# Token projections by strips of 256 x 512, attention probabilities normalised at the output, and two moved waits in a two-layer hybrid backbone kernel

## The reference

```python
p = h @ w_in[li]                                   # one projection for all mixers
def diff_softmax(q, k, v, lam):
    s = einsum('bhqcd,bhkcd->bhcqk', q, k) * (A_DQK ** -0.5)
    p = softmax(s, axis=-1)
    a = p[:, :, 0] - lam * p[:, :, 1]
    return einsum('bhqk,bhkv->bhqv', a, v)
y = rmsnorm(o, subln_w) * (1.0 - lambda_init)      # after attention
mod = silu(c) @ w_ada[li] + b_ada[li]              # shifts, scales and gates
```

## Time and profile before

| what | value |
|---|---|
| median of 3 runs | 2313.76 us (2312.54 to 2314.17) |
| profiled execution, own time | 2313.24 us |
| its span in the profile | 2311.2 us |
| PE, busy share of the span | 94% |
| DVE, ACT, POOL | 51%, 37%, 29% |
| token projections, matmuls of 256 columns | 1344 |

### The profile page before, as it was taken

One profiled execution on the slowest core, in us unless ns is written; L12 is line 12 of the kernel. 1 busy time (PEld: TensorE's weight loads), 2 busy tenths in 40 slices (PEclk: granted clock), 3 DMA queues, 4 the chain that ended last, 5 costly groups with the idle time before them and its releaser, 6 DMA issues.

```text
span 2311.2 us, 36487 instructions
## 1 busy us (share of the span) xinstructions
PE 2171.6 (94%) x13284; PEld 1822.6 (79%) x13284; DVE 1167.6 (51%) x1937; ACT 861.9 (37%) x1655; POOL 671.4 (29%) x607
## 2 busy tenths in 40 slices
PE   6998999999998999999899999899999889998999
PEld 3565788898664888887788888678889767998999
DVE  4745444435567332335543443454555565557665
ACT  2334333232552332333332231354333444444443
POOL 2432222246122111114320123433335433114120
PEclk8999999999999999999999999999999989999999
DMA  7412333322652123233223333220002423554554
GB/s 234 144 46 100 103 99 110 110 93 83 205 183 80 36 92 100 94 96 92 81 92 100 95 97 100 78 73 19 20 19 66 133 69 100 174 178 143 182 182 146
DMA packets 233362, 245.36 MB, mean 106 GB/s; under 512 B 11475, under 2 KB 230036, under 8 KB 232212
## 3 DMA queue, kind: packets, MB, share of 16 engines
q1 hardware_dynamic: 229648, 232.19, 31.9%
q10 hardware_dynamic: 3588, 11.49, 1.4%
HBM read 237.36 MB, written 6.29 MB: 105 GB/s over the span
## 4 chain that ended last, share of the span: by engine, by line
PE 71%; DVE 11%; issue 8%; ACT 4%; POOL 4%; DMA 1%; DVEq 0%; SPq 0%; ACTq 0%; POOLq 0%
PE psum L562 50%; PE psum L557 20%; DVE big L2028 5%; DVE big L2037 2%; PE psum L681 2%; POOL whl L1274 1%; ACT tmp L1478 1%; ACT big L1478 1%; POOL big L2721 1%; DMA raw<-in_w_ada_dram 1%; DVE big L2032 1%; ACT whl L1265 1%; POOL big L2615 1%; ACT big L1481 1%; DVE small L2429 1%
## 5 line engine op out<-in xcount | busy, mean ns | idle before, releaser
L562 PE MATMUL psum<-hhl,whl 128*128 128x512 f32 (+1 forms) x4416 | 828.7, 347 | 27.6 <-DVE hhl L2149 18.4
L562 PEld LDWEIGHTS psum<-hhl,whl 128*128 128x128 f32 x4416 | 702.7, 192 | 154.2 <-issue 43.7
L1265 ACT CAST whl<-raw 128x512 fp32r<-128x512 f32 x656 | 374.3, 618 | 884.7 <-PE psum L562 879.8
L1274 DVE TENSOR_TENSOR whl<-raw,whl 128x512 fp32r<-128x512 f32 x480 | 330.6, 730 | 487.2 <-ACT whl L1265 486.6
L557 PE MATMUL psum<-big 128*128 128x128 f32 (+5 forms) x2944 | 484.4, 328 | 31.9 <-DVEq L1246 13.1
L562 PE MATMUL psum<-bigr,whl 128*128 128x512 f32 (+1 forms) x2688 | 470.0, 336 | 4.7 <-DVEq L2534 2.5
L557 PEld LDWEIGHTS psum<-big 128*128 128x128 f32 (+2 forms) x2944 | 383.1, 195 | 109.4 <-issue 49.7
L562 PEld LDWEIGHTS psum<-bigr,whl 128*128 128x128 f32 x2688 | 414.3, 190 | 57.9 <-issue 4.7
L1274 POOL TENSOR_TENSOR whl<-raw,whl 128x512 fp32r<-128x512 f32 x176 | 230.1, 1329 | 400.5 <-ACT whl L1265 381.7
L1481 ACT COPY big<-psum 128x512 f32<-128x512 f32 (+1 forms) x330 | 184.7, 560 | 292.5 <-PE psum L557 199.8
L2028 DVE TENSOR_TENSOR big<-big,psum 128x512 f32<-128x512 f32 (+1 forms) x166 | 99.2, 598 | 148.0 <-PE psum L557 143.9
(11 more groups left out here) (148 smaller groups left out, 1455.4 us busy)
## 6 DMA issues: line engine op xcount, KB each, us to landing
raw<-in_w_mlp_dram SPq DMA_DIRECT2D x128, 512.0 KB, 3.6
raw<-in_w_ada_dram SPq DMA_DIRECT2D x96, 512.0 KB, 4.6
raw<-in_w_in_dram SPq DMA_DIRECT2D x88, 512.0 KB, 3.6
raw<-in_w_gate_dram SPq DMA_DIRECT2D x64, 512.0 KB, 3.5
raw<-in_w_branch_dram SPq DMA_DIRECT2D x32, 512.0 KB, 3.5
raw<-in_w_o_dram SPq DMA_DIRECT2D x16, 512.0 KB, 3.5
hy_spectra<-big SPq DMA_DIRECT2D x2, 2560.0 KB, 8.5
big<-hy_spectra ACTq DMA_DIRECT2D x2, 1280.0 KB, 5.7
```

What stands on the lines that cost most here:

```text
L562: m = nc.tensor.matmul(o_, a(p_), b(q_), start=first and i == 0, stop=last and i == 2, skip_group_check=shared)
L1265: nc.scalar.copy(whl[:, r, 0, ks], raw_of(n)[:, ks]).then_inc(S["hi_ready"], 1)
L1274: ins = eng.tensor_tensor(whl[:, r, 1, ks], raw_of(n)[:, ks], whl[:, r, 0, ks].bitcast(F32), ALU.subtract)
```

## The change

It has four parts. **First**, a strip of a token projection now has 256 rows and all 512 columns; it is loaded, cast and split in the same two halves of 512 columns. Each matmul moves 512 columns, a projection still takes four strips, and each unit holds one token tile. All units of a projection are opened at its first strip and end in its last one, tile by tile. ACT copies the first three tiles (or all but the last) before the cast that follows the last strip, and the last tile behind it; the woven pieces' two copies both come with the fourth piece. `half_way` runs after the second strip. **Second**, `combine` makes the sum of the first exponential times its factor over that of the second, so that the first exponential stays undivided. The division by its sum is made in `o_copy`, in four ACTIVATE instructions with a scale by head in place of one copy, after a new DVE reciprocal of four sums (`inverse_ready`). **Third**, layer 1's rows go to a part of `rstd`, with a semaphore of their own, and are turned to columns in group 2 of the modulation; DVE copies those columns after `filter_cut(0, 1)`. **Fourth**, in layer 1 POOL waits for `eo_ready` of the second convolution before it makes the low parts for `merge`.

The diff, cut to its core (callers that only lose an argument, DVE's side of `columns`, and the removed bodies of `token_strips` and `woven_piece` are left out):

```diff
...
 modrow = rows[:].rearrange("p a c -> p (a c)")
+rows_of = [rows, None]
...
 rstd = sb("rstd", [P, T])
+rows_of[1] = rstd[:, 0:2 * P].rearrange("p (a c) -> p a c", a=2)
...
-ROWS_DONE = [7 * 16, 12 * 16]
+ROWS_DONE = [7 * 16, 5 * 16]
...
-PAIRS = [(0, 1), (1,)]
+def by_rows(w, off):
+    return [w[STRIP * j:STRIP * (j + 1), off:off + BR_W].rearrange("(k p) n -> p k n", p=P) for j in range(4)]
+def token_tiles(li, key):
+    return range(2, NT) if li and key in ("dz", "aq") else range(NT)
+def add_tokens(key, li, off):
+    n = len(token_tiles(li, key))
+    add(key, li, by_rows(w_in[li], off), [1, 1, 1, n], n)
...
-    np_ = len(PAIRS[li])
...
-        add(key, li, by_columns(w_in[li], off, 512), [1, np_] * 2, 2 * np_)
-    add("ak", li, by_columns(w_in[li], OFF_AK, 512), [1, 2] * 2, 4)
-    add("av", li, by_columns(w_in[li], OFF_AV, 512), [1, 2] * 2, 4)
+        add_tokens(key, li, off)
+    add_tokens("ak", li, OFF_AK)
+    add_tokens("av", li, OFF_AV)
...
+    token_banks = []
+    def token_strip(key, li, j):
+        tl = token_tiles(li, key)
+        assert first_strip[key, li] + j == n_strip[0]
+        w = strip().rearrange("p q (k a) n -> p q k (a n)", k=2)
+        if j == 0:
+            token_banks.clear()
+        for i, m_ in enumerate(tl):
+            if j == 0:
+                token_banks.append(unit())
+            for k in range(2):
+                m = mm3(token_banks[i], lambda p_: hhl[:, p_, 2 * j + k, m_ * P:(m_ + 1) * P],
+                        lambda q_: w[:, q_, k, :], j + k == 0, j == 3 and k == 1)
+            if j == 3 or m_ == NT - 1:
+                m.then_inc(unit_done, 1)
+    def token_strips(key, li):
+        assert first_unit[key, li] == n_unit[0]
+        for j in range(4):
+            token_strip(key, li, j)
...
+        token_strip(key, li, n)
...
+    def columns(li):
+        pe.wait_ge(rows_loaded[li], ROWS_DONE[li])
+        b = fill(("cols", li))
+        nc.tensor.transpose(b[:, 0:100], rows_of[li][0:100, 0, :], ident[0:100, 0:100])
+        n = 52 if li == 0 else 36
+        nc.tensor.transpose(b[:, 128:128 + n], rows_of[li][0:n, 1, :], ident[0:n, 0:n]).then_inc(filled, 1)
...
-        for li in range(DEPTH):
-            pe.wait_ge(rows_loaded, ROWS_DONE[li])
-            if li == 0:
-                pe.wait_ge(consts_loaded, 16)
-            b = fill(("cols", li))
-            nc.tensor.transpose(b[:, 0:100], rows[0:100, 0, :], ident[0:100, 0:100])
-            n = 52 if li == 0 else 36
-            nc.tensor.transpose(b[:, 128:128 + n], rows[0:n, 1, :], ident[0:n, 0:n]).then_inc(filled, 1)
+        pe.wait_ge(consts_loaded, 16)
+        columns(0)
...
                 filter_taps(0, 1)
+                columns(1)
...
-    per = {"dz": len(PAIRS[li]), "aq": len(PAIRS[li])}.get(key, 2)
-    return first_mark[key, li] + (1 + per) * (i // per) + 2 + i % per
+    if key in ("dz", "aq", "ak", "av"):
+        return first_mark[key, li] + 4 + i
+    return first_mark[key, li] + 3 * (i // 2) + 2 + i % 2
...
+def exp_sum(m_, h, cc):
+    c0 = SUMC + (8 + h % 2 if cc else 4 * (m_ % 2) + h)
+    return small[:, c0:c0 + 1]
+def exp_inverse(m_, h, n=1):
+    c0 = SUMC + 12 + 4 * (m_ % 2) + h
+    return small[:, c0:c0 + n]
...
+        to = rows_of[li]
+        for dst, src in ((to[0:48, 0, :], b_ada[li]), (to[48:56, 0, :], norm1[li]),
+                         (to[56:64, 0, :], norm2[li]),
+                         (to[64:100, 0, :], hy_conv[li].rearrange("a c -> (a c)")),
+                         (to[0:36, 1, :], dn_conv[li].rearrange("a c -> (a c)"))):
+            sp.dma_start(dst, src.rearrange("(r c) -> r c", c=P)).then_inc(rows_loaded[li], 16)
...
+            sp.dma_start(rows[36:44, 1, :], c_ctx.rearrange("(r c) -> r c", c=P)).then_inc(rows_loaded[li], 16)
+            sp.dma_start(rows[44:52, 1, :], c.rearrange("a (r c) -> (a r) c", c=P)).then_inc(rows_loaded[li], 16)
...
                 sp.wait_ge(S["lo_ready"], split_no[last] + 1)
-        sp.dma_start(raw_of(n), strips[n]).then_inc(strip_loaded[at % RAW], 16)
+        dst = raw_of(n)
+        if strips[n].shape[1] == 2:
+            dst = dst.rearrange("p (k a) n -> p k (a n)", k=2)
+        sp.dma_start(dst, strips[n]).then_inc(strip_loaded[at % RAW], 16)
...
-                if n % 2:
-                    b = unit_bank_of(act, key, li, n // 2)
-                    dst = dz_tok[:, 2:4] if key == "dz" else y[:, ATT, 0:2]
-                    step(copy(dst[:, :, n // 2 * STRIP:(n // 2 + 1) * STRIP],
-                              b.rearrange("p (m n) -> p m n", m=2)),
-                         act_step if key == "dz" else S["token_copied"])
-                    give_unit(act, key, li, n // 2)
+                for u, m_ in enumerate(tiles(li)) if n == 3 else ():
+                    b = unit_bank_of(act, key, li, u)
+                    if key == "dz":
+                        step(copy(dz_tok[:, m_, :], b))
+                    else:
+                        step(copy(qk_tile(li, 0, m_), b), S["token_copied"])
+                    give_unit(act, key, li, u)
...
-        n, u = first_strip[key, li], 0
-        prs = PAIRS[li] if key in ("dz", "aq") else (0, 1)
-        for s_ in range(2):
-            hi_ahead(act, n + 2 * s_)
-            hi_ahead(act, n + 2 * s_ + 1)
-            for pr in prs:
-                b = unit_bank_of(act, key, li, u)
-                step(f(dst[:, 2 * pr:2 * pr + 2, s_ * STRIP:(s_ + 1) * STRIP],
-                       b.rearrange("p (m n) -> p m n", m=2), fn), S["token_copied"])
-                give_unit(act, key, li, u)
-                u += 1
-            if half_way and s_ == 0:
+        n = first_strip[key, li]
+        for j in range(3):
+            hi_ahead(act, n + j)
+            if half_way and j == 1:
...
+        for u, m_ in enumerate(token_tiles(li, key)):
+            if m_ == NT - 1:
+                hi_ahead(act, n + 3)
+            b = unit_bank_of(act, key, li, u)
+            step(f(dst[:, m_, :], b, fn), S["token_copied"])
+            give_unit(act, key, li, u)
...
-            step(copy(a_o[:, m_, :], b), S["o_copied"])
+            act.wait_ge(S["inverse_ready"], (0 if li == 0 else NT - 2) + m_ + 1)
+            for h in range(HEADS):
+                ins = f(a_o[:, m_, h * P:(h + 1) * P], b[:, h * P:(h + 1) * P], ACT.Identity,
+                        scale=exp_inverse(m_, h))
+            step(ins, S["o_copied"])
...
                        bias=small[:, MAXC + 8 + par:MAXC + 9 + par],
-                       accum_out=small[:, SUMC + par:SUMC + par + 1]), S["exp_ready"])
+                       accum_out=exp_sum(m_, h, cc)), S["exp_ready"])
...
             dve.wait_ge(S["exp_ready"], 2 * n + 2)
-            r = small[:, SUMC + 2 * par:SUMC + 2 * par + 2]
-            step(V.reciprocal(r, r))
-            tt(r[:, 1:2], r[:, 1:2], sm(LAM + 3, 1), MUL)
+            r = small[:, SUMC + 10 + par:SUMC + 11 + par]
+            step(V.reciprocal(exp_sum(m_, h, 1), exp_sum(m_, h, 1)))
+            stt(r, exp_sum(m_, h, 0), sm(LAM + 3, 1), exp_sum(m_, h, 1), MUL, MUL)
...
             ks = slice(0, (2 if m_ < 2 else 4) * P)
-            ts(p[:, 0, ks], p[:, 0, ks], r[:, 0:1], None, MUL)
-            stt(p[:, 0, ks], p[:, 1, ks], r[:, 1:2], p[:, 0, ks], MUL, ADD, S["a_ready"])
+            stt(p[:, 0, ks], p[:, 1, ks], r, p[:, 0, ks], MUL, ADD, S["a_ready"])
+            if h == HEADS - 1:
+                c0 = SUMC + 4 * (m_ % 2)
+                step(V.reciprocal(exp_inverse(m_, 0, HEADS), small[:, c0:c0 + HEADS]), S["inverse_ready"])
...
         add_bias(1)
+        if li:
+            pool.wait_ge(S["eo_ready"], hyz(li, 1, 1) + 1)
...
```

69 lines of the change are left out of this document (16 added, 53 removed).

## The result

| | before | after |
|---|---|---|
| median of 6 runs each | 2313.28 us | 2297.74 us |
| lowest to highest | 2311.14 to 2317.98 | 2292.03 to 2303.02 |
| profiled execution, own time | 2313.24 us | 2292.58 us |
| its span | 2311.2 us | 2290.2 us |

The ratio of the times is 0.9932, with a 95% interval of 0.9917 to 0.9947: the change takes 15.5 us off, 12 to 19 by the interval. The forecast was 2295 us and a gain of 18.8.

A forecast was written before the change was run, and what follows sets the result against it. PE bounds the kernel, busy 94% of the span, directly or waiting for DVE and POOL; 5.7 + 8.1 + 4.5 + 0.5 = 18.8 us off the runs' median gives 2295 us (chance 0.50), range 2285 to 2307 us.

The forecast's parts named there:

- the start: Early load of layer 1's rows: first group at 11 to 13 us, 0.5 us gained (minus 5 to plus 4).
- Wider strips: Token projections of both layers and woven pieces: 512-column matmuls save 13.9 ns a pair, 5.7 us (2 to 8).
- rival (b): Token strips: a matmul costs the skill's columns plus 2.5 ns, strips gain 1 us, 2300 us; chance 0.05.
- Attention: Multiply removed from DVE's chain, mainly layer 1, and clock partly regained: 8.1 us (3 to 11).
- 5.0 + 2.5: Layer 1's attention: 5.0 us from removed multiplies less new reciprocals, 2.5 us (0 to 5) from the clock.
- POOL's wait: Layer 1's Hyena: DVE's row shrinks 3.0 us, the clock gives 2.2, 0.7 off; together 4.5 us (2 to 6).
- Two signs of being right: At the start: the first group before 13 us, and the filter taps near 29 us.
- A third: Sign of being right in layer 0: a longer PE wait before the Hyena projection, 3.34 us becoming some 4.3.
- (d): Start: PE idles 3 to 5 us before the taps, then half speed costs 24 us; 2319 us, chance 0.04.
- (a): Terms hold, but clock not regained in attention and at 1920, or DVE meets POOL elsewhere: 2301 us; chance 0.20.
- (c): Bound passes to PE's own work or ACT in attention, and low parts meet the spectrum product: 2308 us; chance 0.10.
- (e): The start falls the good way, clock and table both: 2288 us; chance 0.11.

The follow-up runs named there:

- the second profile: The changed kernel run once more, unaltered, with its own profile: 2298.54 us, ratio 0.9931.
- the fillers: The changed kernel with unread turns of the identity on PE in six waits of layer 1's attention: 2294.79 us, ratio 0.9905.

## Why the prediction was right, and where it was not

The direction and the size were right: 15.5 us gained of 18.8 forecast, and 2297.74 us lies in the range. The total is nearer to the forecast than its terms are: the start came out 4 us worse than its term, and the parts' medians alone add up to 11.5 us, so that some luck is in it. Point by point:

*Wider strips, 5.7 us forecast.* 6.7 us in the stretches: 4.26 in layer 0, 1.86 in layer 1 up to av's last strips (1.1 in the second profile, 1.7 in the kernel with the strips alone), and 0.55 in these, 11.75 to 11.20 us. By the medians of the kernel with the strips alone it is 5.9 us. The price of a pair, 13.9 ns, came out as 2 x 120.3 - 227.3 = 13.3 ns. So the rule of the Trainium skill that I had weighed (TensorE: Matmul & The Clock Gate, "Wait — 56ns, not 53.3ns?"), 2.5 ns beside the columns, is not what this kernel's stream of matmuls pays, and rival (b) is out. I had sized one thing wrong, to the cautious side: that POOL's row at the end of av would stay and PE's wait grow by 1 us. It grew by 0.10 us.

*Attention, 8.1 us forecast.* The waits of PE for DVE fell to 3.6 us, as said; those of the Hyena turns, which the forecast didn't name, rose by 0.9. By the medians the part gave 4.6 us alone and 3 to 6 in company, by the stretches 7 in layer 1. There the sum came near, 7 us for 5.0 + 2.5, but by the estimate above its two terms did not: about 3 us came from the waits themselves and not 5.0, and about 4 us from the clock and not 2.5. All of the clock came back in one profiled execution of the changed kernel and a part in the other, and the fillers speak for PE's waits as what decides it. In layer 0 nothing can be read from one profile: nine with the part have 206.5 to 213.3 us for that stretch, by how often the clock falls in it (3 to 20 us of half clock), and five without it 209.35 to 211.48. With half of the half clock taken off, the nine have 203.6 us in the mean and the five 203.3, so the 0.6 us forecast there doesn't show. The medians and single executions differ by 2 to 3 us here, and that is not settled: the interval of each median is as wide.

*POOL's wait, 4.5 us forecast.* 5.1 us in the stretch, 3.5 us by the median. DVE's 3.0 us and the clock's 2.2 us came as the rows had them. The 0.7 us that I took off for new collisions was not paid: DVE's next four operations take one operand from PSUM and ran their 0.68 or 0.69 us each beside POOL's low parts. Here the Trainium skill (SBUF — State Buffer, "SBUF: two separate sides") says that DVE and GpSimd share one pair of ports, that this is an exclusive lock, and that of DVE's operations without a faster mode those with two operands in SBUF meet it. This case's traces agree: 1.70 us for each of the three products between SBUF tiles beside POOL, 0.71 us each without it, and 0.68 us beside POOL for the one from PSUM.

*The start, 0.5 us of gain forecast.* This is the step that failed. It cost 3.5 us: dz starts at 460.9 us in the mean of six profiles with this part and no filler there, and at 457.4 us in five without it. By the medians it cost 2.5 us alone, which is not told apart from nothing, and 4.4 to 5.2 in company. The step had named the right pieces, that the table can't come earlier and that the clock may fall; what it left out of the price was that PE's wait in front of the table turns from 0.28 into 2.36 us, and that the clock falls behind such a wait. The range I gave it, minus 5 to plus 4 us, holds the cost. Two signs of being right failed with it: the first group began at 13.45 us and not before 13, and the taps at 30.30 and not near 29. A third was weak: the wait before the Hyena projection of layer 0 grew from 3.34 to 3.44 us only.

*The rivals.* (d) had this mechanism and gave it a chance of 0.04, at a price of 24 us. The mechanism came, and its price was far too high: 10 to 14 us more at half clock lose PE 5 to 7 us of work by estimate, and 3.5 us reached dz. Mechanism and price should have been kept apart: a likely small loss was filed as an unlikely large one. (a) holds in part, in the attention of the second profile. Together with the start that would explain why the median is 2.7 us over the forecast, but no run parts the two. (c) didn't come: ACT's four short divisions take 1.14 us for the old copy's 0.59, and PE's largest waits for ACT over the span are as they were (5.0, 5.0 and 3.7 us in three groups, 5.0, 5.0 and 3.6 before). This is the row of ACT in the changed kernel's timeline:

```profile
703.11 1.14 ACT L1491 ACTIVATE big<-psum,small 128x128 f32<-128x128 f32 x4 [2.98 <-PE psum L566]
```

(e) fell the other way. Its 2288 us, 7 us under the forecast, wasn't worked out either: the range of the start's term allowed 3.5 us, and the clock's in attention 2.5.

The four parts' medians alone add up to 5.9 + 4.6 + 3.5 - 2.5 = 11.5 us, and the whole gives 15.5. Each of these has an uncertainty of about 3 us, so whether the parts help each other is left open.

## What to carry to other kernels

Price a load or a step that comes earlier by what PE does in the time won: if it only waits longer for the next thing, nothing is gained, and the clock can make it a loss. Where PE waits 2 us for something that can't come sooner, a handful of matmuls that nobody reads, into a bank that is free, is worth a try: the four kernels with them gain 4 to 10 us more over the kernel before than the same kernels without them, though the intervals of some overlap and in one of them the half clock only moved. And when the runs of a kernel spread by 10 us, take a second profile before pricing a stretch by one.
